# Seven expert-weight places free earlier, router transposes in the attention output, unnormalised rows gathered

## What is computed

```python
h = rms_norm(x, norm_ffn_g)                       # x * rsqrt(mean(x*x) + eps) * g
g_prob = softmax(h @ w_rg + b_rg); g_idx = argmax(g_prob)        # 4 groups
e_logits = (h @ w_re + b_re) of group g_idx                       # 8 experts in it
top_p, top_i = top_k(softmax(e_logits), 2)        # two experts for each token
# for each expert e, on its tokens:
y = (silu(h @ w1[e]) * (h @ w3[e])) @ w2[e]       # 1024 -> 512 -> 1024
x = x + sum of the token's two y, weighted
```

## Time and profile before

| | |
|---|---|
| median of 3 runs | 1792.56 us |
| lowest, highest | 1787.67, 1798.92 us |
| span of the profiled execution | 1788.7 us |
| PE busy | 1628.3 us (91%) |
| DVE, ACT, POOL busy | 739.1, 482.9, 367.3 us |
| moved by DMA | 328.08 MB |

### The profile page before, as it was taken

One profiled execution on the slowest core, in us unless ns is written; L12 is line 12 of the kernel. 1 busy time (PEld: TensorE's weight loads), 2 busy tenths in 40 slices (PEclk: granted clock), 3 DMA queues, 4 the chain that ended last, 5 costly groups with the idle time before them and its releaser, 6 DMA issues.

```text
span 1788.7 us, 15347 instructions
## 1 busy us (share of the span) xinstructions
PE 1628.3 (91%) x5808; PEld 797.4 (45%) x5808; DVE 739.1 (41%) x1525; ACT 482.9 (27%) x984; POOL 367.3 (21%) x348
## 2 busy tenths in 40 slices
PE   6989999999999798988888887999988999998898
PEld 3434457544555333333333333544446454445553
DVE  2856535353433211101100103379764154996622
ACT  2022242001121100000000002475355135645531
POOL 3700001000000111111011101168043012832500
PEclk9999999999999898999888888989999999999999
DMA  8511023445541999999999999202201210020101
GB/s 327 188 47 48 18 101 141 171 158 200 195 175 75 357 415 402 406 398 417 398 404 407 410 416 345 86 1 71 71 17 73 102 57 1 24 108 11 47 1 47
DMA packets 72977, 328.08 MB, mean 183 GB/s; under 512 B 10522, under 2 KB 13746, under 8 KB 60480
## 3 DMA queue, kind: packets, MB, share of 16 engines
q1 hardware_dynamic: 64976, 310.23, 44.7%
q0 software_dynamic: 6144, 10.52, 1.8%
q10 hardware_dynamic: 1776, 6.27, 0.9%
HBM read 320.60 MB, written 14.78 MB: 187 GB/s over the span
## 4 chain that ended last, share of the span: by engine, by line
PE 70%; DMA 19%; DVE 8%; ACT 1%; issue 1%; POOL 0%; ACTq 0%; SPq 0%; POOLq 0%; DVEq 0%
PE bank L187 66%; DMA arena<-in_w 15%; DMA arena<-h_rows,arena 3%; DVE arena L2552 1%; DVE arena L2536 1%; PE bank L2150 1%; PE bank L581 1%; DVE arena L2593 1%; DVE arena L2606 1%; DMA arena<-y_rows 0%; DMA arena<-in_params 0%; PE bank L906 0%; PE bank L664 0%; PE bank L2097 0%; DMA y_rows<-arena 0%
## 5 line engine op out<-in xcount | busy, mean ns | idle before, releaser
L187 PE MATMUL bank<-arena 128*128 128x512 f32 (+10 forms) x4944 | 1524.4, 551 | 87.0 <-DMA arena<-in_w 49.6
L187 PEld LDWEIGHTS bank<-arena 128*128 128x128 f32 (+5 forms) x4944 | 693.9, 179 | 849.3 <-issue 784.3
L2768 POOL TENSOR_TENSOR arena<-arena 128x512 f32<-128x512 f32 x180 | 205.3, 1141 | 224.1 <-ACT arena L2377 206.3
L1798 DVE TENSOR_TENSOR arena<-arena,bank 64x512 f32<-64x512 f32 x32 | 22.1, 691 | 314.3 <-ACT arena L1222 314.3
L1852 POOL TENSOR_TENSOR arena<-arena 128x1 f32<-128x1 f32 (+2 forms) x44 | 32.8, 745 | 565.5 <-DVE arena L1256 338.4
L2377 ACT ACTIVATE arena<-arena 128x512 f32<-128x512 f32 x180 | 126.1, 717 | 21.5 <-POOL arena L2768 21.4
L990 ACT COPY arena<-bank 128x512 f32<-128x512 f32 (+3 forms) x115 | 61.1, 538 | 246.6 <-PE bank L187 146.8
L1222 ACT ACTIVATE arena<-bank 64x512 f32<-64x512 f32 x32 | 18.9, 591 | 368.9 <-PE bank L187 368.9
L1873 POOL DMA_INDIRECT y_rows<-arena x32 | 32.1, 1004 | 412.8 <-PE bank L906 258.9
L1266 DVE SCALAR_TENSOR_TENSOR arena<-arena 128x512 f32<-128x512 f32 x84 | 78.4, 934 | 3.0
L1791 DVE TENSOR_TENSOR arena<-bank,arena 128x512 f32<-128x512 f32 x32 | 22.1, 692 | 111.3 <-PE bank L906 111.3
(11 more groups left out here) (264 smaller groups left out, 897.4 us busy)
## 6 DMA issues: line engine op xcount, KB each, us to landing
arena<-in_w SPq DMA_DIRECT2D x96, 2048.0 KB, 40.0
arena<-in_w_in SPq DMA_DIRECT2D x15, 2048.0 KB, 9.0
arena<-in_w_ada SPq DMA_DIRECT2D x12, 2048.0 KB, 9.0
arena<-in_w_out SPq DMA_DIRECT2D x6, 2048.0 KB, 7.6
arena<-in_w_xk SPq DMA_DIRECT2D x2, 2048.0 KB, 9.4
arena<-in_w_xv SPq DMA_DIRECT2D x2, 2048.0 KB, 10.9
arena<-in_w_xq SPq DMA_DIRECT2D x2, 2048.0 KB, 9.8
arena<-in_w_xo SPq DMA_DIRECT2D x2, 2048.0 KB, 9.0
```

The lines of the kernel that those rows point to most:

```text
L187: i = pe.e.matmul(o, l, r, start=first and j == 0, stop=last and j == len(pairs) - 1)
L2768: pool.e.tensor_tensor(yc, yc, k.prod[l][n % 4], ALU.add).then_inc(*k.pool.step("sum", l, f, j))
```

## The change

The places that the first ten expert loads take are in another order, with `features` and `router` first. That needs `k.HT` and the router's scratch free earlier. So the router's transposes go into slices of `k.OT` whose product with `w_xo` is done, the squares write their unused output there too, and the router's small tensors move out of the `router` place. The rows are stored to `h3_rows` no more: the gathers read `x_rows`, where the raw x stands, and the root, a positive factor for each row, is applied behind the products, as the scale of the Silu and as a factor of the multiplication after it. The root of each row of an expert comes from the product that makes the token lists, which is 64 columns wide instead of 32. Two waits of SP (for the last store to `h3_rows`, and for the first two gathers) fall away. The overflow path reads the roots from a small table in device memory, `root_rows`.

```diff
+    k.RS = k.AH[:, 0, :]
...
-    R.ends[features] = [(P, ("lg", 2))]
-    R.ends[router] = [(P, ("slot",)), (k.h3_out[0], ("h3", 2)), (k.h3_out[1], ("h3", 3))]
-
-    R.ends[residual] = [(k.x_out, ("x", 3)), (k.act, ("sq", "f", 3)), (k.act, ("xn", "f", 3)), (P, ("tr", 3, 1))]
-    R.go_on([ring[2], ring[3], tokens, cross, ring[4], ring[0], ring[1], features, residual, router])
+    R.ends[features] = [(P, ("qx", 7))]
+    R.ends[router] = [(P, ("xv", 3, 1))]
+    R.ends[residual] = [(k.x_out, ("x", 3)), (k.act, ("sq", "f", 3)), (P, ("tr", 3, 1))]
+    R.go_on([features, router, tokens, cross, ring[2], ring[3], ring[4], ring[0], ring[1], residual])
...
-            if e == 2:
-
-                sp.wait_ge(*k.h3_out[1].done("h3", 3))
-            expert("w3", e, 8, 512, "up")
-            if e == 2:
-                for j in range(2):
-                    sp.wait_ge(*k.xg_in[j].done(j))
             if e == 0:
                 sp.wait_ge(*P.done("xs", 7))
                 sp.e.dma_start(k.WR, chunks(k.a["w_router"], 8)).then_inc(*k.wr_in.step("w"))
+            expert("w3", e, 8, 512, "up")
...
-def act_row_store(k, act, t):
-
-    act.wait_ge(*k.pool.done("root", "f", t))
-    act.e.activation(k.XNf[t % 2], k.X[:, t, :], ACT.Copy, scale=k.f_ss[:, t:t + 1]).then_inc(*k.act.step("xn", "f", t))
-    act.wait_ge(*k.act.last())
-    act.e.dma_start(k.h3_d[t * 128:(t + 1) * 128, :], k.XNf[t % 2]).then_inc(*k.h3_out[t % 2].step("h3", t))
...
+    if u == 0:
+        act.wait_ge(*k.dve.done("gg", 1, 1))
     act_copy(k, act, k.LR[:, t * 128:end * 128], k.banks.at("lg", u)[:, 0:(end - t) * 128], "lg", u)
...
+            act.wait_ge(*V.done("rs"))
+            act.e.activation(k.hs[e % 2][0:BLK, :], k.banks.at("up", e)[0:BLK, :], ACT.Silu,
+                             scale=k.RS[0:BLK, e:e + 1]).then_inc(*A.step("up", e))
...
+                for t in range(4):
+                    act.e.dma_start(k.rs_d[t * 128:(t + 1) * 128, :], k.f_ss[:, t:t + 1]).then_inc(*k.rs_out.step("root", t))
...
+    root = k.f_ss[:, t0:end].unsqueeze(2).unsqueeze(3).broadcast_to([128, n, 2, 32])
+    i = dve.e.tensor_tensor(k.AHV[:, 2 * t0:2 * end, 32:64].rearrange("p (t j) e -> p t j e", t=n),
+                            AH.rearrange("p (t j) e -> p t j e", t=n), root, ALU.mult)
...
+    dve.e.tensor_copy(k.RS[0:64, :], b[0:64, 32:64]).then_inc(*V.step("rs"))
...
-    dve.e.tensor_tensor(hs, hs, k.banks.at("up", e)[64:128, :], ALU.mult).then_inc(*k.dve.step("up", e))
+    dve.e.scalar_tensor_tensor(out=hs, in0=hs, scalar=k.RS[0:BLK, e:e + 1], in1=k.banks.at("up", e)[64:128, :],
+                               op0=ALU.mult, op1=ALU.mult).then_inc(*k.dve.step("up", e))
...
-        out=k.xg[j][0:BLK, :], out_offset=None, in_=k.h3_d,
+        out=k.xg[j][0:BLK, :], out_offset=None, in_=k.x_d,
...
-    for t in (2, 3):
-        pool.wait_ge(*k.h3_out[t % 2].done("h3", t))
+    pool.wait_ge(*k.x_out.done("x", 3))
```

More of the change, by code:

```diff
@@ L216, in build @@
         k.view = view
-        k.h3_d = nc.dram_tensor("h3_rows", [T, D], F32).ap()
+        k.rs_d = nc.dram_tensor("root_rows", [T, 1], F32).ap()
         k.x_d = nc.dram_tensor("x_rows", [T, D], F32).ap()
@@ L228, in build @@
         k.bg_in, k.gfin_in, k.wr_in = (count(n, 16) for n in ("bg_in", "gfin_in", "wr_in"))
-        k.h3_out = [count(f"h3_out{j}", 16) for j in range(2)]
+        k.rs_out = count("rs_out", 16)
         k.tab, k.scat, k.ki_in = (count(n, 16) for n in ("tab", "scat", "ki_in"))
@@ L382, in memory @@
     assert at[0] <= base + 5876
-    at[0] = base + 17140
-    k.AH, k.AHV, k.PP = next_(8, 32), next_(8, 32), next_(8, 32)
+    at[0] = base + 5632
     k.ELT = next_(4, 32)
-    assert at[0] <= base + 18164
-    at[0] = base + 18164
+    k.GI, k.EI = next_(4, 8).bitcast(U32), next_(4, 8).bitcast(U32)
+    k.OHG = next_(4, 4)
+    k.gif = next_(4)
+    assert at[0] <= base + 5876
+    lr_at = base + 18164
+    k.LR, k.PP = view(lr_at, 512), view(lr_at, 8, 32)
+    at[0] = lr_at
+    k.NB, k.NT, k.CU = next_(32), next_(32), next_(32)
+    k.xe, k.xb = next_(16), next_(16)
+    at[0] = lr_at + 512
+    k.AH, k.AHV = next_(8, 32), next_(8, 64)
+    k.XC = view(lr_at + 768, NX, 32)
+    k.RS = k.AH[:, 0, :]
     k.LG = next_(4, 40)
     k.GM, k.EM = next_(4, 8), next_(4, 8)
-    k.GI, k.EI = next_(4, 8).bitcast(U32), next_(4, 8).bitcast(U32)
-    k.gif, k.gw, k.ex, k.dn4 = next_(4), next_(4), next_(4), next_(4)
-    k.GE, k.OHG = next_(4, 4), next_(4, 4)
+    k.gw, k.ex, k.dn4 = next_(4), next_(4), next_(4)
+    k.GE = next_(4, 4)
     k.EL, k.EID = next_(4, 8), next_(4, 2)
+    k.IDA = k.EL.rearrange("p t e -> p (t e)")
     k.AS, k.ASP = next_(4, 32), next_(5, 32)
@@ L397, in memory @@
     k.DSTU, k.SIDU = next_(8).bitcast(U32), next_(8).bitcast(U32)
[L398 to L402, removed]
+    k.CN = next_(32)
+    assert at[0] <= base + 20105
+    k.RXS = small(1)
     both = view(base + 256, 3, 4096)
@@ L832, in pe_router_logits @@
             pe.wait_ge(*(k.act.done("tr", end - 1, 0) if c < 4 else k.dve.done("tr", end - 1, 1)))
-            i = product(pe, b[64 * m:64 * m + 64, 0:n], [(k.WR[:, c, :], k.HT[:, c, cols])],
+            i = product(pe, b[64 * m:64 * m + 64, 0:n], [(k.WR[:, c, :], k.OT[:, c, cols])],
                         first and j == 0, last and j == len(pairs) - 1)
@@ L862, in pe_router_slots @@
     pairs = [(k.OHS[:, q, :], k.AHV[:, q, :]) for t in GROUPS[u] for q in (2 * t, 2 * t + 1)]
-    i = product(pe, b[:, 0:32], pairs, u == 0, u == 2)
+    i = product(pe, b[:, 0:64], pairs, u == 0, u == 2)
     if u == 2:
@@ L1146, in act_cross @@
                 act_copy(k, act, k.OT[:, 2 * h + 1, :], B.at("xv", h, 1), "xv", h, 1)
[L1149 to L1154 removed]
 def act_router_squares(k, act, t):
+    free = (t if t < 3 else 0) * 128
     act.wait_ge(*k.dve.done("o", "w_xo", t, 1))
[L1159 to L1161 removed]
+    act.e.activation(k.OT[:, :, free:free + 128], k.X[:, t, :].rearrange("p (c s) -> p c s", c=8), ACT.Square,
+                     accum_out=k.f_ss[:, t:t + 1]).then_inc(*k.act.step("sq", "f", t))
 def act_router_turn(k, act, t):
[L1165 removed]
+    if t < 3:
+        act.wait_ge(*k.act.done("sq", "f", t))
+    act_copy(k, act, k.OT[:, 0:4, t * 128:(t + 1) * 128], k.banks.at("tr", t, 0).rearrange("p (f s) -> p f s", f=4), "tr", t, 0)
 def act_router_logits(k, act, u):
     t, end = GROUPS[u][0], GROUPS[u][-1] + 1
+    if u == 0:
+        act.wait_ge(*k.dve.done("gg", 1, 1))
     act_copy(k, act, k.LR[:, t * 128:end * 128], k.banks.at("lg", u)[:, 0:(end - t) * 128], "lg", u)
@@ L1227, in act_first @@
                 act.e.activation(k.ex, k.ex, ACT.Exp).then_inc(*A.step("ex"))
+                act.wait_ge(*k.pool.done("root", "f", 3))
+                for t in range(4):
+                    act.e.dma_start(k.rs_d[t * 128:(t + 1) * 128, :], k.f_ss[:, t:t + 1]).then_inc(*k.rs_out.step("root", t))
         if e:
@@ L1719, in dve_router @@
                                op1=ALU.add).then_inc(*V.step("idx"))
+    dve.e.tensor_copy(k.RS[0:64, :], b[0:64, 32:64]).then_inc(*V.step("rs"))
     dve.e.tensor_scalar(k.IDY, b[:, 0:32], 2.0, C("high2"), ALU.mult, ALU.add).then_inc(*V.step("slot"))
+    dve.e.memset(k.RXS, 0.0)
+    dve.e.memset(k.TAB, 2 * T).then_inc(*V.step("tab"))
 def dve_router_weights(k, dve, part):
@@ L1911, in pool_first @@
         pool_root(k, pool, k.f_ss[:, t:t + 1], "f", t)
-    pool.wait_ge(*P.done("o", "w_xo", 3, 1))
+    pool.wait_ge(*P.done("lg", 2))
     for j in range(2):
@@ L1946, in overflow @@
     sp.wait_ge(*k.scat.done(7))
+    pool.wait_ge(*k.rs_out.done("root", 3))
     pe.wait_ge(*A.done("dn", NE - 1))
@@ L1975, in overflow @@
                 pool.e.indirect_dma_start(
-                    out=xg, out_offset=None, in_=k.h3_d,
+                    out=xg, out_offset=None, in_=k.x_d,
                     in_offset=bass.IndirectOffsetOnAxis(ap=k.IXR[0:BLK, 1:2], axis=0), bounds_check=T - 1,
                     oob_is_err=False).then_inc(o["gather"], 16)
-                pe.e.wait_ge(o["gather"], 16 * x + 16)
+                pool.e.indirect_dma_start(
+                    out=k.RXS[0:BLK, :], out_offset=None, in_=k.rs_d,
+                    in_offset=bass.IndirectOffsetOnAxis(ap=k.IXR[0:BLK, 1:2], axis=0), bounds_check=T - 1,
+                    oob_is_err=False).then_inc(o["gather"], 16)
+                pe.e.wait_ge(o["gather"], 32 * x + 32)
                 if x:
@@ L1997, in overflow @@
                 act.e.wait_ge(o["pe"], 4 * x + 2)
-                act.e.activation(hs, bu[0:BLK, :], ACT.Silu).then_inc(o["act"], 1)
+                act.e.activation(hs, bu[0:BLK, :], ACT.Silu, scale=k.RXS[0:BLK, :]).then_inc(o["act"], 1)
                 dve.e.wait_ge(o["act"], 2 * x + 1)
-                dve.e.tensor_tensor(hs, hs, bu[64:128, :], ALU.mult).then_inc(o["dve"], 1)
+                dve.e.scalar_tensor_tensor(out=hs, in0=hs, scalar=k.RXS[0:BLK, :], in1=bu[64:128, :], op0=ALU.mult,
```

(1 more changed line is left out.)

22 lines of the change are left out of this document (9 added, 13 removed).

## The result

| | before | changed |
|---|---|---|
| median | 1795.43 us (4 runs) | 1810.14 us (4 runs) |
| lowest, highest | 1787.67, 1798.92 | 1806.78, 1814.36 |
| span of the profiled execution | 1788.7 | 1806.5 |

The ratio is 1.010, with a 95% interval of 1.0075 to 1.0124: the change makes the kernel slower, by 15 us between the medians. The forecast was 5.9 us faster. None of its named cases and not its range of 1779 to 1796 us reaches as far as 1810.

A forecast was written before the change was run, and what follows sets the result against it. The prediction took the stream of expert weight loads to bound the stage: 6.1 us gained at the eleventh load, 0.2 lost after the last `up`, so -5.9 us; median 1792.56 to 1786.7 us, range 1779 to 1796.

The forecast's parts named there:

- named cases: Forecast 1786.7 us (chance 0.58) and rivals from 1782.1 to 1795.2 us; all lie within 13 us.
- The step that failed: Stage of the experts: the four stores of roots cost 0, at most one load's 5 us.
- What bounds the kernel: Stage of the experts: it ends when the stream of weight loads ends, about 400 GB/s, 96 loads of 2 MB.
- The places: Seven loads fit well before 580, eighth and ninth issue at 580.18; ten places full at 599, eleventh waits for `up` 0.
- The end of `up` 0: Expert 0's product `up`: ends at 610.3 instead of 609.56, 0.7 us later through the gathers.
- the two rivals on gathers and store: First gathers: colliding fully, 1792.2 us, chance 0.18; or delayed by a late store of x, 1795.2 us, chance 0.07.
- A collision of the gathers: Gathers 0 and 1 beside ninth and tenth loads; at worst 10.9 us each, as gather 3 took.
- the middle that was taken: First gathers' delay: 0.7 us, between ending 1.3 us later and at the same time.
- The gain of 6.1 us: Eleventh load: lands at 617.8 instead of 623.9, meeting an empty queue, and the gain is kept to the end.
- The router: Before the gathers: new waits and products cost 0 us; rival that it gets 4.6 us shorter, 1782.1 us, chance 0.09.
- ACT's relief: Router: ACT loses four tile multiplications and four stores; no gain on the path, as ACT idled 2.01 us for PE.
- The Silu with a factor from memory: Steps for each expert: the Silu takes a factor from memory instead of 1.0, price 0.

The follow-up runs named there:

- hold_two_loads: Changed kernel, root stores moved into the overflow branch, SP's ninth load waiting for x's last store, tenth for gathers 0 and 1: 1785.83 us, ratio 0.9962.

## Why the prediction was wrong, step by step

- **The step that failed**: "The four stores of roots, 512 pieces of 4 bytes, run beside the stream with nobody waiting but the overflow branch ... I take 0, and at most one load's 5 us". It measured 21.0 us on the changed kernel and 25.8 on the one before. I asked who waits for the stores, and not what they do to the resource that bounds the stage. The upper bound had no row behind it; the text said that no row has such a piece being stored, and then gave a bound all the same.
- **What bounds the kernel** was right: what was late at the 94th load came out in the time. It landed 20.1 us later, and the span grew by 17.8; the stretch behind it was 2.3 us shorter, which is inside what it varies by (710.9 to 714.4 us over the profiles here).
- **The places** did what was said: seven loads out by 524, two at 580.77, then a hole from 601 to 614. That the eleventh load waits for `up` 0 was right.
- **The end of `up` 0**: 30.1 us after the start was forecast, 32.8 measured. The store of x was sized by a row with 5.3 us beside the tail of one load; with two whole loads beside it it took 11.15. It landed at 592.65, between the two loads and not behind both. That was 0.6 us after the table was there, and the first gather took 8.5 where 0.7 us more than 5.8 was allowed. This is the mechanism of the two rivals on gathers and store, each at part of its price. A collision of the gathers was bounded by the 10.9 us of the earlier trace rows; the middle that was taken was too low.
- **The gain of 6.1 us** can be had once these two are kept apart: hold_two_loads has 6.3. That the two numbers are so close is in part luck. `up` 0 ends 28.6 us after the start there, 1.5 earlier than forecast, and the twelfth load lands 13.9 us after `up` 0 instead of the 12.6 forecast.
- **The router** was as long as before: the new waits were covered, and ACT's relief gave nothing, as said (12.2 us to the first gather in hold_two_loads, 12.1 before). The Silu with a factor from memory was priced at 0; it takes 684 ns for 591, and DVE's multiplication 750 for 691. That is 0.15 us an expert: 0.06 of DVE's, for which up to 0.24 were allowed, and 0.09 of the Silu's, for which nothing was. It doesn't show in the stream.

## What to carry to other kernels

In a stage that is bound by DMA, ask of every added transfer what it does to the other transfers, not only who waits for it; 2 KB in the wrong form cost as much as four loads of 2 MB. The share of the engines' time that it takes is no measure of that: it was 0.7% here. A column of small elements written out side by side is such a form: space the destinations (64 bytes were enough here), or write it only where it is needed. And a prefetch that fills all places ahead of a fixed release gains only what the release allows; there its last loads can be held back for the short transfers on the critical chain, at no price.

## What the runs showed of the hardware

- 4-byte pieces stored side by side from ACT's queue halve the rate of a stream of loads as long as they last (about 200 for 405 GB/s); the same pieces 64 bytes apart do not. The pieces' own packets take 9 ns each; packets of the loads are held up to 5.1 us. Why is not shown: that neighbours are written one after another at one place in memory is a guess that no run tests, and that the price is 6.6 us from the loads' own queue and 21 from another stays unexplained.
- A store of 0.5 MB took 2.6 us alone, 8.7 beside one load of 2 MB and 11.15 beside two; at the stream's 405 GB/s its bytes are 1.3 us.
- POOL's queue sent the same four stores as 64 packets of 32 bytes, ACT's as 512 of 4 bytes.
- One store of 128 such pieces took 8.5 us to land with no load beside it, 6.5 of them after the last piece had been sent.
